# Unscaled residual to the router, and norm, scale and shift put on gathered rows by ScalarE

## What is computed

```python
x = x + g1 * _rms_norm(y, norm_g[1])                 # y: mixer output
h2 = _modulate(_rms_norm(x, norm_g[2]), sh2, sc2)    # h * (1 + scale) + shift
x = x + g2 * _rms_norm(_moe(h2, ...), norm_g[3])

def _moe(h, router_w, w_gate, w_up, w_down):
    top_v, top_i = lax.top_k(h @ router_w, 2)        # 2 of 8 experts a token
    top_w = jax.nn.softmax(top_v, axis=-1)
    ... sum over experts of gate * (silu(h @ wg) * (h @ wu)) @ wd, inner width 2816
```

## Time and profile before

| | |
|---|---|
| median of 3 executions | 1693.77 us (1692.86 to 1694.52) |
| span of the profiled execution, first to last instruction | 1690.2 us |
| what lies around the span, against the median | 3.6 us |
| TensorE matmul busy | 1630.1 us, 96% of the span |
| VectorE busy | 1058.0 us, 63% |
| ScalarE busy | 934.1 us, 55% |
| mean granted TensorE clock | 0.988 |
| router stage, from the last output piece to the first expert matmul | 893 to 923 us |
| expert stage | 923 to 1680 us |

### The profile page before, as it was taken

How to read it: one execution, slowest core, us unless ns; L and a number is a source line. 1 busy time by engine, 2 the same in 40 slices (tenths; PEclk the granted TensorE clock), 3 DMA queues, 4 the chain that set the end, 5 groups by cost and what they waited for, 6 DMA issues and landing times.

```text
span 1690.2 us, 22690 instructions
## 1 busy us (share of the span) xinstructions
PE 1630.1 (96%) x8402; PEld 1302.9 (77%) x8402; DVE 1058.0 (63%) x1356; ACT 934.1 (55%) x1336; POOL 37.6 (2%) x60
## 2 busy tenths in 40 slices
PE   6999999899999999899998999999999999999998
PEld 2785469798888888688685888888888888888886
DVE  3352332442222333553655889999999989999998
ACT  4413422542222333552564777777877777787775
POOL 0000000040000000000001000000000000000000
PEclk9999999999999999999998999999999999999998
DMA  8513672686222222352124999999999999999992
GB/s 342 203 75 122 227 299 76 228 340 254 100 100 100 100 100 98 130 212 100 51 110 171 420 396 386 386 369 383 364 398 363 402 360 395 377 371 395 365 346 76
DMA packets 67705, 426.24 MB, mean 252 GB/s; under 512 B 8624, under 2 KB 12464, under 8 KB 19760
## 3 DMA queue, kind: packets, MB, share of 16 engines
q1 hardware_dynamic: 59856, 396.93, 61.1%
q0 software_dynamic: 7776, 28.32, 4.3%
HBM read 401.62 MB, written 23.59 MB: 252 GB/s over the span
## 4 chain that ended last, share of the span: by engine, by line
PE 90%; DVE 4%; ACT 3%; DMA 2%; issue 1%; SPq 0%; ACTq 0%; DVEq 0%
PE ps L1662 26%; PE ps L1664 26%; PE ps L1663 26%; PE ps L1680 2%; PE ps L1705 2%; PE ps L1822 1%; PE ps L2133 1%; DMA raw<-in_w 1%; DMA x<-in_x 1%; DVE small L1211 1%; PE ps L1883 1%; ACT raw L536 1%; PE ps L1866 1%; DVE raw L1377 0%; PE ps L1855 0%
## 5 line engine op out<-in xcount | busy, mean ns | idle before, releaser
L1509 DVE TENSOR_TENSOR wl<-raw,wh 128x1024 fp32r<-128x1024 f32 x522 | 615.8, 1222 | 63.6 <-ACT wh L911 56.5
L911 ACT ACTIVATE wh<-raw 128x1024 fp32r<-128x1024 f32 x522 | 524.8, 1057 | 97.6 <-PE ps L1664 97.6
L1662 PE MATMUL ps<-wh,ah 128*128 128x512 f32 (+1 forms) x800 | 311.0, 389 | 1.7 <-ACT ah L894 1.2
L1662 PE MATMUL ps<-ah,wh 128*128 128x512 f32 (+1 forms) x848 | 301.7, 356 | 7.8 <-DVE al L1122 3.3
L1664 PE MATMUL ps<-wh,al 128*128 128x512 f32 (+1 forms) x800 | 302.4, 378 | 0.0
L1663 PE MATMUL ps<-wl,ah 128*128 128x512 f32 (+1 forms) x800 | 301.7, 377 | 0.0
L1663 PE MATMUL ps<-al,wh 128*128 128x512 f32 (+1 forms) x848 | 293.6, 346 | 0.0
L1664 PE MATMUL ps<-ah,wl 128*128 128x512 f32 (+1 forms) x848 | 293.5, 346 | 0.0
L1007 DVE TENSOR_TENSOR wl<-raw,wh 128x1024 fp32r<-128x1024 f32 x120 | 141.6, 1222 | 130.2 <-ACT wh L493 130.2
L1662 PEld LDWEIGHTS ps<-ah,wh 128*128 128x128 f32 x848 | 161.3, 190 | 35.0 <-issue 9.1
L1663 PEld LDWEIGHTS ps<-al,wh 128*128 128x128 f32 x848 | 161.4, 190 | 20.6 <-issue 0.7
(11 more groups left out here) (251 smaller groups left out, 1504.5 us busy)
## 6 DMA issues: line engine op xcount, KB each, us to landing
raw<-in_w SPq DMA_DIRECT2D x372, 1024.0 KB, 6.8
sent<-raw POOLq DMA_DIRECT2D x16, 512.0 KB, 24.6
back<-raw POOLq DMA_DIRECT2D x16, 512.0 KB, 25.3
x<-sent POOLq DMA_DIRECT2D x7, 512.0 KB, 12.3
back<-x POOLq DMA_DIRECT2D x7, 512.0 KB
x<-in_x SPq DMA_DIRECT2D x1, 2048.0 KB, 13.5
raw<-in_ukv SPq DMA_DIRECT2D x1, 1024.0 KB, 7.4
out<-raw SPq DMA_DIRECT2D x4, 256.0 KB, 3.0
```

The source lines that it names most:

```text
L911: act.activation(wh[:, J % SPLITS, piece_half(h)], slot(J % SLOTS)[:, piece_half(h)], ACT.Copy).then_inc(w_hi, 1)
L1509: ins = dve.tensor_tensor(wl[:, J % SPLITS, piece_half(h)], slot(J % SLOTS)[:, piece_half(h)], wh[:, J % SPLITS, piece_half(h)].bitcast(F3 ...
L1662: pe.matmul(out, lh, rh, start=start, stop=False)
```

## The change

The router's matmuls and the transposes now read the residual `x` itself; the gain and scale are multiplied into the router's weights once (on VectorE, far earlier). The token's square sum is taken by ScalarE from the turned rows in PSUM, with an accumulator, and the root is a small one per token. The scattered rows hold x times root only. Gain, scale and shift are put on after the gather: ScalarE makes for every expert eight ACTIVATEs (Identity, 128x128, scale and bias both read per partition) into a buffer, waits for them, and rounds the buffer in two ACTIVATEs of 128x512; VectorE subtracts in two pieces. The post-norm gain and gate of the mixer go into the evacuation of its output (two 128x256 with a scale in place of one 128x512), so that the residual is done in pairs of chunks. The shift's spreading (`diag`, eight matmuls, `shiftB`) goes. Slots 3 and 10 of `raw` are loaded when the residual is done; slot 10 waited for the token rows before.

```diff
-        diag = sq[:, :, :].rearrange("p a (b c) -> p (a b) c", c=P)
+        xe_first = [sq[:, h, :] for h in range(2)]
+        xe_next = [rope[:, :, :].rearrange("p a b -> p (a b)"), rinv[:, :]]
...
+        tok_ss, tok_sum = small[:, 64:70].rearrange("p (t n) -> p t n", t=2), small[:, 72:74]
+        ss_parts = ((0, 4), (4, 6), (6, KD))
+
+        def turned(t, a, b):
+            bank, first = (2 * t, 0) if a < 4 else (2 * t + 1, 4) if a < 6 else (7 - 3 * t, 6)
+            return ps[:, bank, (a - first) * P:(b - first) * P]
...
-                if j == EARLY_SLOTS:
-                    sp.wait_ge(res_done, RES_BEFORE[N_O2])
-                if j == SLOTS - 1:
-                    sp.wait_ge(sem("tok_f32"), len(tok_parts))
+                if j in (EARLY_SLOTS, SLOTS - 1):
+                    sp.wait_ge(res_done, RES_ALL)
...
                 if p == 0:
-                    act.wait_ge(sem("shift_ps"), 1)
-                    act.activation(shiftB.rearrange("p a b -> p (a b)"), ps[:, 6:8, :].rearrange("p a b -> p (a b)"),
-                                   ACT.Copy).then_inc(sem("shift_ready"), 1)
+                    act.wait_ge(sem("last_scales"), 1)
                 act.wait_ge(w_used, s + 1)
                 bank = evac_banks(("t", p))[0]
                 squares(N_OY, lambda k: ps[:, bank + k % 2, 0:TL], chunks=(2 * p, 2 * p + 1))
-                act.activation(y_o[:, 2 * p:2 * p + 2, :], ps[:, bank:bank + 2, 0:TL], ACT.Copy).then_inc(evac_act, 1)
+                for k in (2 * p, 2 * p + 1):
+                    ins = act.activation(y_o[:, k, :], ps[:, bank + k % 2, 0:TL], ACT.Copy, scale=scl[:, 1, 1, k, 0:1])
+                ins.then_inc(evac_act, 1)
                 if p in (1, 2):
                     first_split(p - 1)
             root(N_OY)
-            for k in range(KD):
-                squares(N_O2, lambda k: x[:, k, 0:TL], lambda k: act.wait_ge(res_done, 4 * KD + k + 1), chunks=(k,))
-                act.activation(scaled_x[:, k, :], x[:, k, 0:TL], ACT.Copy, scale=scl[:, 1, 2, k, 0:1]).then_inc(sem("x_scaled"), 1)
-
-
-            root(N_O2)
+
+
+            for n, (a, b) in enumerate(ss_parts):
+                act.wait_ge(sem("tok_ps"), n + 1)
+                for t in range(2):
+                    act.activation(tok[:, t, a * P:b * P], turned(t, a, b), ACT.Square, accum_out=tok_ss[:, t, n:n + 1]).then_inc(sem("tok_squared"), 1)
+            act.wait_ge(sem("tok_summed"), 1)
+            act.activation(tok_rinv, tok_sum, ACT.Ln, bias=eps[:, 0:1], scale=1.0 / D).then_inc(sem("tok_ln"), 1)
+            act.wait_ge(sem("tok_ln"), 1)
+            act.activation(tok_rinv, tok_rinv, ACT.Exp, scale=-0.5).then_inc(sem("tok_root"), 1)
+            act.wait_ge(sem("tok_root"), 1)
+            for t, h in tok_parts:
+                for a, b in ss_parts[h:2 * h + 1]:
+                    ins = act.activation(tok[:, t, a * P:b * P], turned(t, a, b), ACT.Copy, scale=tok_rinv[:, t:t + 1])
+                ins.then_inc(sem("tok_f32"), 1)
...
+            def modulated(v, k):
+
+                act.activation(v[k // 4][:, (k % 4) * P:(k % 4 + 1) * P], ps[:, 6 + k // 4, (k % 4) * P:(k % 4 + 1) * P], ACT.Identity,
+                               bias=mod1[:, 24 + k, 0:1], scale=scl[:, 1, 2, k, 0:1]).then_inc(sem("xe_v"), 1)
+
+            def rounded(v, h):
+                return act.activation(xeh[:, 4 * h:4 * h + 4, :].rearrange("p a b -> p (a b)"), v[h], ACT.Copy)
+
             def first_gathered():
 
-                for h in range(2):
-                    act.wait_ge(sem("first_ps"), h + 1)
-                    act.activation(xeh[:, 4 * h:4 * h + 4, :].rearrange("p a b -> p (a b)"), ps[:, 6 + h, :], ACT.Copy
-                                   ).then_inc(sem("first_xe_h"), 1)
+                for k in range(KD):
+                    act.wait_ge(sem("first_ps"), k // 4 + 1)
+                    modulated(xe_first, k)
+                    if k % 4 == 3:
+                        act.wait_ge(sem("xe_v"), k + 1)
+                        rounded(xe_first, k // 4).then_inc(sem("first_xe_h"), 1)
 
             def gathered(count):
                 act.wait_ge(sem("xe_ps"), count)
-                act.activation(xeh[:, :, :].rearrange("p a b -> p (a b)"),
-                               ps[:, 6:8, :].rearrange("p a b -> p (a b)"), ACT.Copy).then_inc(sem("xe_h"), 1)
+                for k in range(KD):
+                    modulated(xe_next, k)
+                act.wait_ge(sem("xe_v"), KD * count + KD)
+                rounded(xe_next, 0)
+                rounded(xe_next, 1).then_inc(sem("xe_h"), 1)
...
+            link(dve.tensor_tensor(router, router, scl[:, 1, 2, :, 0:1].broadcast_to([P, KD, NE]), ALU.mult))
             scale_post(1, 3, 40).then_inc(sem("last_scales"), 1)
...
-                if p == 7:
-                    dve.tensor_tensor(diag, ident[:, None, :].broadcast_to([P, KD, P]),
-                                      mod1[:, 24:24 + KD, 0:1].broadcast_to([P, KD, P]), ALU.mult).then_inc(sem("diag_ready"), 1)
...
-            residual(N_OY, lambda k: y_o[:, k, :], 1, 1)
-
-
-            inverse(N_O2)
+            inverse(N_OY)
+            pair = lambda v: v.rearrange("p (a b) -> p a b", a=2)
+            for p in range(KD // 2):
+                if p >= 2:
+                    dve.wait_ge(res_done, RES_BEFORE[N_OY] + p - 1)
+                two = slice(2 * p, 2 * p + 2)
+                counted(N_OY, p, dve.tensor_tensor(pair(tmp[p % 2]), y_o[:, two, :], rinv[:, None, 0:TL].broadcast_to([P, 2, TL]), ALU.mult))
+                dve.wait_ge(t_ready, T_AT[N_OY, p] + 1)
+                dve.tensor_tensor(x[:, two, 0:TL], x[:, two, 0:TL], pair(tmp[p % 2]), ALU.add).then_inc(res_done, 1)
+
+
+            dve.wait_ge(sem("tok_squared"), 2 * len(ss_parts))
+            dve.tensor_reduce(tok_sum, tok_ss, AX.X, ALU.add).then_inc(sem("tok_summed"), 1)
             dve.wait_ge(sem("logits_ps"), 1)
-            dve.tensor_tensor(logit_rows, ps[0:NE, 5, 0:TL], rinv[0:NE, 0:TL], ALU.mult).then_inc(sem("logit_rows"), 1)
-            dve.wait_ge(sem("logits_T"), 1)
-            link(dve.tensor_tensor(L, ps[:, 6, 0:16].rearrange("p (t e) -> p t e", t=2), shift_logits[:, None, :].broadcast_to([P, 2, NE]), ALU.add))
+            dve.wait_ge(sem("tok_root"), 1)
+            for t in range(2):
+                ins = dve.scalar_tensor_tensor(out=L[:, t, :], in0=ps[:, 5 + t, 0:NE], scalar=tok_rinv[:, t:t + 1], in1=shift_logits,
+                                               op0=ALU.mult, op1=ALU.add)
+            link(ins)
             link(dve.tensor_reduce(top, L, AX.X, ALU.max))
             dve.tensor_scalar(neg_top, top, -1.0, None, ALU.mult).then_inc(sem("top_ready"), 1)
-            dve.tensor_copy(tok_rinv, ps[:, 6, 16:18]).then_inc(sem("tok_rinv"), 1)
...
-            dve.wait_ge(sem("mask_ready"), 1)
-            dve.wait_ge(sem("shift_ready"), 1)
-            dve.wait_ge(sem("tok_ps"), 1)
-            dve.wait_ge(sem("tok_rinv"), 1)
-
-            def tokens(t, h):
-                dve.scalar_tensor_tensor(out=tok[:, t, 512 * h:512 * h + 512], in0=ps[:, 2 * t + h, :], scalar=tok_rinv[:, t:t + 1],
-                                         in1=shiftB[:, 2 * h:2 * h + 2, :].rearrange("p a b -> p (a b)"), op0=ALU.mult, op1=ALU.add
-                                         ).then_inc(sem("tok_f32"), 1)
-
-            for t, h in tok_parts[0:2]:
-                tokens(t, h)
             dve.wait_ge(sem("rank_ps"), 1)
-            link(dve.scalar_tensor_tensor(out=flat(rank), in0=ps[:, 4, 16:32], scalar=1.0, in1=flat(picked), op0=ALU.add, op1=ALU.mult))
+            link(dve.scalar_tensor_tensor(out=flat(rank), in0=ps[:, 6, 16:32], scalar=1.0, in1=flat(picked), op0=ALU.add, op1=ALU.mult))
             for t in range(2):
                 ins = dve.tensor_scalar(sel[:, t, :], iota, rank[:, t, 0:1], -1.0, ALU.subtract, ALU.is_equal)
             ins.then_inc(sem("sel_ready"), 1)
-            for t, h in tok_parts[2:4]:
-                tokens(t, h)
             dve.wait_ge(sem("rank_ps"), 2)
             dve.tensor_reduce(cnt[:, :], ps[:, 5, 32:40], AX.X, ALU.max).then_inc(sem("count_ready"), 1)
...
-                    part = slice(4 * h, 4 * h + 4)
-                    dve.tensor_tensor(flat(xel[:, part, :]), ps[:, 6 + h, :], flat(xeh[:, part, :]).bitcast(F32), ALU.subtract
-                                      ).then_inc(sem("first_xe_l"), 1)
+                    remainder(xe_first, h).then_inc(sem("first_xe_l"), 1)
+
+            def remainder(v, h):
+                part = slice(4 * h, 4 * h + 4)
+                return dve.tensor_tensor(flat(xel[:, part, :]), v[h], flat(xeh[:, part, :]).bitcast(F32), ALU.subtract)
 
             def gathered(count):
                 dve.wait_ge(sem("xe_h"), count)
-                dve.tensor_tensor(flat(xel[:, :, :]), ps[:, 6:8, :].rearrange("p a b -> p (a b)"), flat(xeh[:, :, :]).bitcast(F32),
-                                  ALU.subtract).then_inc(sem("xe_l"), 1)
```

(28 more changed lines are left out.)

21 lines of the change are left out of this document (10 added, 11 removed).

## The result

| | before | after |
|---|---|---|
| median (lowest to highest), 4 executions each | 1693.32 us (1690.73 to 1694.52) | 1719.45 us (1717.22 to 1720.02) |
| ratio, 95% interval | | 1.0152 (1.0140 to 1.0164) |
| span of the profiled execution | 1690.2 us | 1718.4 us |

The account below looks back on a forecast made before the run. TensorE bounds the expert stage (busy 99.93 of 100 us), a chain through three engines the router stage. Terms -2 - 3.8 - 0.3 + 22.4 + 13 = +29.3 us on span 1690.2, with 3.6 around it: 1723.1 us, range 1707 to 1735.

Parts of the forecast that it names:

- Part 1: Expert loop, seven gathers: ScalarE's eight modulations and two roundings delay TensorE's next expert by 3.2 us each, +22.4 us.
- Part 2: Expert stage: TensorE's granted clock falls behind most of the seven stalls, +13 us (0 to 23).
- Part 3: Attention's end: without the shift's eight matmuls the last head sums and output pieces come earlier, -2 us (-0.9 to -2.5).
- Part 4: Residual to logits: cheaper router chunks on TensorE bring the logits earlier, -3.8 us (-3.2 to -4.8).
- Part 5: Logits to first expert matmul: VectorE, rid of its token parts, is free earlier for its low part, -0.3 us (0 to -0.6).
- The distance around the span: Outside the profiled span: 3.6 us added to the forecast span to compare with the median.
- no stall: Expert loop: the down pieces cover the longer chain, only the early gains stay, 1687.7 us; chance 0.03.
- The clock that holds: Expert stage: dense matmuls keep the clock at 1.00 behind each stall, +16.3, 1710 us; chance 0.16.
- The clock low for the long stretch at each gather: Expert stage: the clock falls at every gather for the 6.83 us stretch, +39, 1733 us; chance 0.11.

## Why the prediction was right

Slower by 26.1 us was measured and 29.3 forecast; 1719.45 lies in the range. The mechanism, a stall in front of each next expert and a clock that falls behind most of them, is what the runs show. By its steps:

- **Part 1, ScalarE's gather: right, with its reason.** 4.00 us against 4.08, a gap of 3.21 against 3.3, +21.9 us against +22.4. The modulations follow each other after 0.35 us (four from 1006.57 to 1007.96) against 0.36. By the Trainium skill (ScalarE: Activation LUTs, What ACT_TABLE_LOAD costs) the eight were an estimated 3.2 us; the trace gives 2.94, wait included, so the rows of before were nearer. The run with modulations gone shows that it is they, the one with plain copies how much of it is the operands.
- **Part 2, the clock: right mechanism, a size off.** 10.2 us against 13. The term took three short stretches, three long ones and none once; it was six short ones and none once. The long stretch was taken over from the earlier trace rows of the router stage, 6.83 us from 896.09; in the loop no gap of 3.2 us brought one (12 low stretches in two kernels, all of 3.41 us). Why the router's was longer isn't shown. The run with modulations twice has the long one, at 6.1 us. The run with the stall filled gives the clock's part directly, 9.5 us.
- **Part 3, attention's end: -2.8 against -2**, just past its end of -2.5. The eight matmuls are 1.1 us at the full clock (31.16 - 30.10, run with them put back) and 1.8 at the low one (32.86 - 31.04); the low clock itself is another 0.9. The term counted the eight, but not that the clock might hold without them. In five of the nine kernels of the same code it didn't, and the term comes out at -1.8 us there. So the -2.8 of this pair is in part chance.
- **Part 4, residual to logits: -5.6 against -3.8**, outside the -3.2 to -4.8. The step that failed is the price of a chunk: 1.38 us at the low and 0.75 at the full clock, where 1.17 and 0.61 were measured. Eight at the low price are 11.0 us; they took 8.2 (898.79 to 907.02), five of them wholly at the low clock. No run shows logits at the 907 to 908.6 that the term is taken from, which is 13.1 to 14.7 us behind the last output piece; over the nine kernels with this code they come 12.1 to 12.5 us behind it, a gain of 5.4 to 5.8 us. A product of 8 columns takes 0.35 us at the low clock (two from 901.47 to 902.18), not the 0.45 taken from the earlier trace rows. The clock stayed low through them, for 17.1 us. The tail took 1.45 us (907.02 to 908.47).
- **Part 5: -0.4 against -0.3**, right.
- **The distance around the span**, 3.6 us, was taken as fixed. It is 1.6 (both kernels), and the other 2.0 were chance in the one profiled execution. The span of 1690.2 and the 3.6 enter as a sum, so this did no harm.

The rivals: no stall (1687.7 us) is close to what the kernel gives once the chain is moved (1686.02), but not as it was written. The clock that holds (1710) is what the run with the stall filled shows (1707.86). The clock low for the long stretch at each gather came only with the doubled chain. All five terms miss to the same side (by 0.5, 2.8, 0.8, 1.8 and 0.1 us), so the sum per stage, +23.2, is 6 us below the forecast; the medians, at +26.1, are 3 us below it. That the forecast comes so near is in part luck, since the 2.9 between the two belong to none of its terms.

## What to carry to other kernels

Count the instructions that stand between the last input and the wait of the bound engine, not their elements: eight ACTIVATEs of 128 columns with two per-partition operands cost 2.9 us, the one rounding of 1024 columns that stood there before 0.9, and each microsecond counted seven times. Before giving up such a change, look at where in the order the chain starts: one exchange in ScalarE's loop took back 25 of the 26 us, and starting it five pieces earlier, with VectorE's two jobs exchanged, made the change the gain of 7 us that its early stages had bought. And price a stall of TensorE as stall plus clock: here 22 and 10 us.

## What the runs showed of the hardware

- The granted clock at gaps of different length between the 128x512 matmuls of the expert stage: at gaps of 0.6, 1.3 and 1.8 us it never fell (0 of 7 each), at 2.08 us in two of seven, at 3.21 us in six of seven (in each of two kernels), at 6.13 us in all seven. The cost steps with it, from 0 to 1.7 and about 2.3 us a fall. Why one gap of 3.21 us goes free isn't shown by these runs, and at the attention's end the clock fell in only five of nine kernels of the same code.
- A fall comes late: TensorE resumes at 2.4 GHz at 1015.45 and is slow only from 1016.4. Over the six falls of the kernel after this is 0.2 to 1.5 us, and over those with the eight matmuls back 0.0 to 1.2. So the slow matmuls stand where nothing waits, and only the granted clock explains them.
- The clock stayed low through the router's chunks: pairs of transposes and 8-column matmuls kept TensorE busy in the records from 898.8 to 907.0, the clock fell among them at 900.3 and stayed at 1.2 GHz until 917.4, through 3.5 us of idle time (907.0 to 910.5) and 5 us of the gather of expert 0's rows (912.3 to 917.4). All ten kernels with this code have the 17.1 us. At 0.61 us a chunk the eight would take 4.9 us; they took 8.2, so up to 3.3 us of the gain in this stage were given back.
